# Two more k-tile pairs with seven block products in the down projection, and the first gain moved behind them

## The chip, the cores and the metric

The kernel runs on one core of one Trainium2 chip. The metric is the device time of one execution in microseconds (us); three runs of the kernel before gave 2082.16, 2082.45 and 2082.65 us, median 2082.45. The profile is of a further execution that took 2081.73 us, of which 2079.9 us lie between its first and its last instruction (the span).

## The reference, cut to what matters

One decoder layer on 256 tokens with a model width of 2048: a SwiGLU feed-forward block (FFN), token mixing, and a second FFN. The change is in the FFN, which runs twice with different weights:

```
D_MODEL, SEQ, D_FF = 2048, 256, 5632

def rmsnorm(x, g):
    return x * rsqrt(mean(x * x) + EPS) * g

def swiglu(x, wg, wu, wd):
    return (silu(x @ wg) * (x @ wu)) @ wd      # wd: 5632 x 2048

f = swiglu(rmsnorm(h, pre_g), wg, wu, wd)
h = h + 0.5 * rmsnorm(f, post_g)
```

All is float32. The part `... @ wd` is called the down stage here.

## The kernel before, in words

**Three passes for one product.** Each float32 operand is split in two parts for TensorE, a rounded one (`_hi`) and the rest (`_lo`), and a product takes three matmuls: hi by hi, lo by hi, hi by lo. ScalarE (ACT) makes the rounded part of a weight slab (`hi`, L517: `whi<-raw`), VectorE (DVE) the rest of it (`lo`, L957: `wlo<-raw,whi`), and TensorE (PE) takes both (`slab`, L1544).

**Slabs and the ring.** A weight slab is two k-tiles of 128 rows by 512 columns, 512 KB. `raw`, `whi` and `wlo` have four slots each, so a load may start when `lo` of the slab four back is done, and `hi` of a slab must wait until PE has used the slab four back (`mm_done`).

**The down stage.** The 5632 hidden rows are 44 k-tiles, or 22 k-tile pairs, numbered q. The 2048 output columns are four chunks of 512. The first half of the stage takes chunks 0 and 1 with q from 0 to 21, two slabs for each q; the second half takes chunks 2 and 3. I number the slabs of the stage from 0 in the order of loading, so q = 20 and q = 21 of the first half are slabs 40 to 43, and the second half starts with slab 44.

**Seven products in place of eight.** For one q, two token tiles by two column chunks by two k-tiles are eight block products of three matmuls, 24 in all. For the q in `DOWN_SEVEN` (9, 11, ..., 19) a scheme of the Strassen-Winograd kind does with seven, 21 matmuls. For that it needs sums of the activations (`down_sum`, split in `down_hi` and `down_lo`, made once for each q and used in both halves) and sums of the weights: four additions on DVE (`weight_sums`, L1150 to L1155), the rounded part on ACT (`wsum_hi`, L688) and the rest on DVE (`down_wsum_lo`, L1159). Four of the seven products go to extra banks (M1, M5, M6, M7), and after the last such q `outer_copies` (ACT, L693 and L694), `combine` (DVE, L1165 to L1171) and `combine_last` (DVE, L1177) put them together in `comb`.

**The order in the second half.** `FRONT` lists the q that are taken for both chunks together: 0, then a plain q and a seven in turn, (1, 9), (2, 11), ..., (6, 19), so 13 of them. `REST` holds the other nine. They are taken for chunk 2 and then for chunk 3, one slab each; the last four slabs of chunk 3 are taken by token tile (`last_slabs`).

**The gain.** The two finished chunks 0 and 1 wait in `comb`. `gain` (DVE, L1245) multiplies them by `gpost` into `fout`, and `squares_of` (ACT, L700) squares them in place for the norm. In the kernel before that is done at i = 3 to 6 of `FRONT`. `comb` must be free before `outer_copies(1)` writes it.

**What sets the order.** Each engine has its own instruction list, written out by hand, and works through it in that order. An engine that waits on a semaphore holds back all that stands behind. No scheduler moves anything.

Of the kernel before, what the change touches and what calls it, by code (L numbers as in the profile page):

```python
# [40 lines left out]
SK = 2  # L41
# [45 lines left out]
SEVEN = (1, 3, 5)  # L87
SUMMED = UP_CHUNKS - 1
DOWN_SEVEN = (9, 11, 13, 15, 17, 19)
PLAIN = [q for q in range(DOWN_SLABS) if q not in DOWN_SEVEN]  # L90
FRONT = PLAIN[:1] + [q for two in zip(PLAIN[1:], DOWN_SEVEN) for q in two]
REST = [q for q in PLAIN if q not in FRONT]
HALF_SLABS = 2 * DOWN_SLABS
REST2, REST3 = HALF_SLABS + 2 * len(FRONT), HALF_SLABS + 2 * len(FRONT) + len(REST)
CONVERT = {0: (0,), 1: (1,), 2: (2,), 3: (3, 4), 4: (5,), 5: (6,), 6: (7,), 7: (8,), 8: (9,), 10: (10,)}
SEVENS = len(SEVEN) * SUMMED + 2 * len(DOWN_SEVEN)
ASUMS = len(SEVEN) + len(DOWN_SEVEN)
COMBINES = SUMMED + 2
SCRATCH = 2048
M1, M5, M6, M7 = range(4)  # L100
# [5 lines left out]
def build(nc, x, rel_bias, f1_wg, f1_wu, f1_wd, f1_post, w_in, b_gate, w_o, conv_dw,  # L106
# [6 lines left out]
    with ctx:  # L113
# [389 lines left out]
        def _(act):  # L503
# [100 lines left out]
            def ffn(f):  # L604
# [71 lines left out]

                def quad(half, n, q):

                    if q in DOWN_SEVEN:
                        seven = down_seven(f, half, DOWN_SEVEN.index(q))  # L680
                    hi_at(n)
                    if q in DOWN_SEVEN:
                        act.wait_ge(wsum_ready, 4 * seven + 3)
                    hi_at(n + 1)
                    if q in DOWN_SEVEN:
                        act.wait_ge(wsum_ready, 4 * seven + 4)
                        act.wait_ge(wsum_used, seven)
                        nc.scalar.activation(wsum_hi[:], wsum[:], ACT.Copy).then_inc(wsumhi_ready, 1)  # L688

                def outer_copies(half):  # L690

                    act.wait_ge(wsum_used, down_seven(f, half, len(DOWN_SEVEN)))
# [10 lines left out]
                for q in range(DOWN_SLABS):  # L703
                    for c in CONVERT.get(q, ()):
                        act.wait_ge(hf_ready, UP_CHUNKS * f + c + 1)
                        nc.scalar.activation(h_hi[:, KB * c:KB * c + KB, :], h_f[:, KB * c:KB * c + KB, :],
                                             ACT.Copy).then_inc(hhi_ready, 1)
                    quad(0, 2 * q, q)
                    if q == 1:
                        gate_silu(SUMMED)  # L710
                    if q == 5:
                        hidden_copy(SUMMED, 0)
                    for c in CONVERT.get(q, ()):
                        if 2 * c + 1 in DOWN_SEVEN:
                            i = DOWN_SEVEN.index(2 * c + 1)
                            act.wait_ge(asum_ready, ASUMS * f + len(SEVEN) + i + 1)
                            nc.scalar.activation(down_hi[:, i], down_sum[:, i], ACT.Copy).then_inc(asumhi_ready, 1)
                    if q == DOWN_SEVEN[-1] + 1:
                        outer_copies(0)
                for i, q in enumerate(FRONT):  # L720
                    quad(1, HALF_SLABS + 2 * i, q)
                    if i == 4:
                        squares_of(0, C11)
                    if i == 6:
                        squares_of(1, C12)
                for k in range(len(REST)):
                    hi_at(REST2 + k)
                    if k == 1:
                        outer_copies(1)
                for k in range(len(REST)):  # L730
                    hi_at(REST3 + k)
# [212 lines left out]
        def _(dve):  # L944
# [162 lines left out]
            def ffn(f):  # L1107
# [117 lines left out]
                def hidden_sums_lo(c):  # L1225
# [23 lines left out]

                def quad(half, n, q, between=None):  # L1250

                    if q in DOWN_SEVEN:
                        seven = down_seven(f, half, DOWN_SEVEN.index(q))
# [288 lines left out]
        def _(pe):  # L1542
# [88 lines left out]
            def ffn(f):  # L1631
# [352 lines left out]
```

## Time and profile before

| | us | |
|---|---|---|
| profiled execution | 2081.73 | span 2079.9 |
| PE busy | 2067.6 | 99% of the span, 9322 matmul records |
| PE weight load | 1711.2 | 82%, lies beside the matmuls |
| DVE busy | 1680.6 | 81% |
| ACT busy | 1111.2 | 53% |
| mean granted PE clock | | 0.999 |
| chain that ended last | | PE 95%, of it L1544 (all the products) 93% |

The busy times overlap. The chain is the work that ended last, followed back step by step to what released it. PE takes up almost all of it.

### The profile page before, as it was taken

What the parts mean: (1) busy time and instruction counts of PE and PEld (TensorE: products, weight loads), DVE (VectorE), ACT (ScalarE), POOL (GpSimd) and SP (SyncE); (2) the same over time, 40 slices, a digit from 0 to 9 for tenths busy, and PEclk for the clock granted to TensorE, in tenths of its full rate; (3) what the DMA queues carried; (4) which work ended last, traced back from release to release, by engine and by line L of the source; (5) the groups of instructions that cost most, each with busy time, mean ns of one, the idle gap of its engine ahead of it and who ended that gap; (6) DMA issues with size and microseconds to landing.
All of it is one profiled execution on the core that took longest, in us unless ns stands there. A gap on an engine that the chain in (4) does not pass through costs nothing.

```text
span 2079.9 us, 25938 instructions
## 1 busy us (share of the span) xinstructions
PE 2067.6 (99%) x9322; PEld 1711.2 (82%) x9322; DVE 1680.6 (81%) x2049; ACT 1111.2 (53%) x1252; POOL 27.7 (1%) x54
## 2 busy tenths in 40 slices
PE   9999999999999999999999999999999999999998
PEld 8888888888888788888788888888888888888886
DVE  6889889889887658998687555578898888889885
ACT  6555555556555454444556444465555555565453
POOL 0000000000000000100000000000000000000000
PEclk9999999999999999999999999999999999999999
DMA  8666556666666566776655666556566665656564
GB/s 287 220 200 205 192 191 202 202 201 193 203 195 215 171 185 191 207 202 179 177 175 175 187 191 209 192 174 208 187 202 201 202 202 187 209 190 208 197 202 162
DMA packets 211996, 409.51 MB, mean 197 GB/s; under 512 B 15114, under 2 KB 15378, under 8 KB 211521
## 3 DMA queue, kind: packets, MB, share of 16 engines
q1 hardware_dynamic: 209904, 401.26, 60.4%
q0 software_dynamic: 1856, 7.01, 1.4%
q8 instruction: 56, 0.92, 0.2%
q14 instruction: 36, 0.29, 0.0%
q10 hardware_dynamic: 144, 0.04, 0.0%
HBM read 406.14 MB, written 2.11 MB: 196 GB/s over the span
## 4 chain that ended last, share of the span: by engine, by line
PE 95%; DVE 2%; DMA 1%; issue 1%; ACT 0%; SPq 0%; POOL 0%; DVEq 0%; ACTq 0%; POOLq 0%
PE banks L1544 93%; PE banks L1594 2%; DVE wlo L957 1%; DMA raw<-in_ffn_wu_dram 1%; DVE res L1012 0%; DMA raw<-in_ffn_wg_dram 0%; DVE act_lo L1025 0%; DVE wsum L1150 0%; DVE wsum L1155 0%; ACT act_hi L532 0%; ACT whi L517 0%; DVE nat L1138 0%; POOL stat L430 0%; DVE comb L1169 0%; DVE comb L1165 0%
## 5 line engine op out<-in xcount | busy, mean ns | idle before, releaser
L517 ACT ACTIVATE whi<-raw 128x1024 fp32r<-128x1024 f32 x755 | 779.7, 1053 | 734.6 <-PE banks L1544 372.1
L957 DVE TENSOR_TENSOR wlo<-raw,whi 128x1024 fp32r<-128x1024 f32 x756 | 900.2, 1218 | 258.9 <-ACT whi L517 255.8
L1544 PE MATMUL banks<-whi,act_hi 128*128 128x512 f32 x1688 | 541.7, 395 | 0.8 <-DVE wlo L957 0.7
L1544 PE MATMUL banks<-whi,act_lo 128*128 128x512 f32 x1688 | 532.0, 389 | 0.0
L1544 PE MATMUL banks<-wlo,act_hi 128*128 128x512 f32 x1688 | 522.3, 389 | 0.1
L1544 PEld LDWEIGHTS banks<-whi,act_lo 128*128 128x128 f32 x1688 | 316.9, 188 | 66.8
L1544 PEld LDWEIGHTS banks<-wlo,act_hi 128*128 128x128 f32 x1688 | 316.7, 188 | 66.7 <-DVE wlo L957 1.0
L1544 PEld LDWEIGHTS banks<-whi,act_hi 128*128 128x128 f32 x1688 | 313.6, 188 | 67.2 <-issue 4.7
L1544 PE MATMUL banks<-whi,h_hi 128*128 128x512 f32 x560 | 179.2, 390 | 0.0
L1544 PE MATMUL banks<-whi,h_lo 128*128 128x512 f32 x560 | 179.0, 389 | 0.0
L1544 PE MATMUL banks<-wlo,h_hi 128*128 128x512 f32 x560 | 174.9, 389 | 0.0
L1544 PEld LDWEIGHTS banks<-whi,h_lo 128*128 128x128 f32 x560 | 105.2, 188 | 21.9
L1544 PEld LDWEIGHTS banks<-wlo,h_hi 128*128 128x128 f32 x560 | 105.1, 188 | 21.7
L1544 PEld LDWEIGHTS banks<-whi,h_hi 128*128 128x128 f32 x560 | 105.0, 188 | 21.6
L1159 DVE TENSOR_TENSOR wsum_lo<-wsum,wsum_hi 128x1536 fp32r<-128x1536 f32 x60 | 105.2, 1753 | 0.0
L1316 DVE SCALAR_TENSOR_TENSOR conv_out<-conv_in,dwt,conv_out 128x256 f32<-128x256 f32 x240 | 100.4, 482 | 0.0
L656 ACT ACTIVATE wsum_hi<-wsum 128x1536 fp32r<-128x1536 f32 x60 | 88.4, 1473 | 0.0
L1150 DVE TENSOR_TENSOR wsum<-raw 128x512 f32<-128x512 f32 x84 | 58.0, 690 | 34.3 <-DMA raw<-in_ffn_wu_dram 18.9
L1152 DVE TENSOR_TENSOR wsum<-wsum,raw 128x512 f32<-128x512 f32 x84 | 58.1, 692 | 2.9
L642 ACT ACTIVATE h_f<-banks 128x1024 f32 (+1 forms) x22 | 22.6, 1025 | 67.8 <-PE banks L1594 67.8
L1165 DVE TENSOR_TENSOR comb<-comb,banks 128x512 f32<-128x512 f32 x24 | 16.5, 688 | 52.1 <-ACT comb L666 40.7
L1155 DVE TENSOR_TENSOR wsum<-wsum,raw 128x512 f32<-128x512 f32 x84 | 57.5, 685 | 0.0
(239 smaller groups left out, 2017.7 us busy)
## 6 DMA issues: line engine op xcount, KB each, us to landing
raw<-in_ffn_wg_dram SPq DMA_DIRECT2D x176, 512.0 KB, 3.7
raw<-in_ffn_wu_dram SPq DMA_DIRECT2D x176, 512.0 KB, 4.6
raw<-in_ffn_wd_dram SPq DMA_DIRECT2D x176, 512.0 KB, 4.7
raw<-in_w_in_dram SPq DMA_DIRECT2D x160, 512.0 KB, 3.6
raw<-in_w_out_dram SPq DMA_DIRECT2D x32, 512.0 KB, 3.6
raw<-in_w_pw_dram SPq DMA_DIRECT2D x16, 512.0 KB, 3.7
raw<-in_w_o_dram SPq DMA_DIRECT2D x16, 512.0 KB, 3.7
x_t<-in_x_tiles_dram SPq DMA_DIRECT2D x8, 256.0 KB, 6.7
```

The costliest lines, as they stand in the source:

```text
L517: nc.scalar.activation(whi[:, j % RING, 0:kts * width], raw[:, j % RING, 0:kts * width], ACT.Copy).then_inc(hi_ready, 1)
L642: nc.scalar.activation(h_f[:, bass.ds(KB * c, KB), :], spare_blocks(group), ACT.Copy).then_inc(hf_ready, 1)
L656: nc.scalar.activation(wsum_hi[:], wsum[:], ACT.Copy).then_inc(wsumhi_ready, 1)
L957: nc.vector.tensor_tensor(wlo[:, j % RING, 0:n], raw[:, j % RING, 0:n], whi[:, j % RING, 0:n], ALU.subtract).then_inc(lo_ready, 1)
L1150: nc.vector.tensor_tensor(wsum[:, P_SUM, :], b11, b12, ALU.add).then_inc(wsum_ready, 1)
L1152: nc.vector.tensor_tensor(wsum[:, R_SUM, :], wsum[:, P_SUM, :], b22, ALU.add).then_inc(wsum_ready, 1)
L1155: nc.vector.tensor_tensor(wsum[:, Z_SUM, :], wsum[:, R_SUM, :], b21, ALU.add).then_inc(wsum_ready, 1)
L1159: nc.vector.tensor_tensor(low[:], wsum[:], wsum_hi[:], ALU.subtract).then_inc(wsumlo_ready, 1)
L1165: nc.vector.tensor_tensor(comb[:, C12, :], comb[:, C11, :], banks[:, b + M6, :], ALU.add).then_inc(combined, 1)
L1316: ins = nc.vector.scalar_tensor_tensor(out=dst, in0=src, scalar=dwt[:, c, w:w + 1], in1=dst, op0=ALU.mult, op1=ALU.add)
L1544: return nc.tensor.matmul(o, a, b, **kw)
L1594: ins = nc.tensor.transpose(dst[:, block0 + k, t * P:(t + 1) * P], src[:, t, k * P:(k + 1) * P], ident[:])
```

## The change

For the second half of the columns only, q = 5 and q = 7 are taken with seven products too, after the six that were. Their activation sums get new buffers (`extra_sum`, `extra_hi`, `extra_lo`, and `extra_full` for hi plus lo of the hidden rows) in the memory that `fout` of chunks 0 and 1 uses. They are made during q = 20 and q = 21 of the first half. `FRONT` grows from 13 to 17 (its new end is 10, 5, 12, 7) and `REST` shrinks from nine to five (14, 16, 18, 20, 21). Gain and squares of chunks 0 and 1 move behind the last seven, into `REST`, and `combine` from the second to the fourth slab of `REST`.

```diff
+EXTRA = (5, 7)
+SEVEN_OF = (DOWN_SEVEN, DOWN_SEVEN + EXTRA)
-PLAIN = [q for q in range(DOWN_SLABS) if q not in DOWN_SEVEN]
-FRONT = PLAIN[:1] + [q for two in zip(PLAIN[1:], DOWN_SEVEN) for q in two]
+PLAIN = [q for q in range(DOWN_SLABS) if q not in SEVEN_OF[1]]
+FRONT = PLAIN[:1] + [q for two in zip(PLAIN[1:], SEVEN_OF[1]) for q in two]
...
@@ scalar (ACT), first half, at the end of the loop over q
                     if q == DOWN_SEVEN[-1] + 1:
                         outer_copies(0)
+                    if q >= DOWN_SLABS - len(EXTRA):
+                        i = q - DOWN_SLABS + len(EXTRA)
+                        act.wait_ge(asum_ready, ASUMS * f + len(SEVEN) + len(DOWN_SEVEN) + i + 1)
+                        nc.scalar.activation(extra_hi[:, i], extra_sum[:, i], ACT.Copy).then_inc(asumhi_ready, 1)
                 for i, q in enumerate(FRONT):
                     quad(1, HALF_SLABS + 2 * i, q)
-                    if i == 4:
-                        squares_of(0, C11)
-                    if i == 6:
-                        squares_of(1, C12)
                 for k in range(len(REST)):
                     hi_at(REST2 + k)
-                    if k == 1:
+                    if k == 2:
+                        squares_of(0, C11)
+                        squares_of(1, C12)
+                        act.wait_ge(squared, 2 * TT * BLK * f + 2 * TT)
                         outer_copies(1)
...
@@ vector (DVE)
+                def extra_sums(i):
+                    q = EXTRA[i]
+                    link(nc.vector.tensor_tensor(extra_full[:, i], h_hi[:, SK * q:SK * q + SK, :], h_lo[:, SK * q:SK * q + SK, :],
+                                                 ALU.add))
+                    a11, a12, a21, a22 = (extra_full[:, i, k, t * P:(t + 1) * P] for t in range(TT) for k in range(2))
+                    link(nc.vector.tensor_tensor(extra_sum[:, i, S5, :], a21, a22, ALU.subtract))
+                    nc.vector.tensor_tensor(extra_sum[:, i, S7, :], a11, a21, ALU.subtract)
+                    link(nc.vector.tensor_tensor(extra_sum[:, i, S6, :], extra_sum[:, i, S5, :], a11, ALU.subtract))
+                    nc.vector.tensor_tensor(extra_sum[:, i, S3, :], extra_sum[:, i, S6, :], a12, ALU.add).then_inc(asum_ready, 1)
+
+                def extra_sums_lo(i):
+                    dve.wait_ge(asumhi_ready, ASUMS * f + len(SEVEN) + len(DOWN_SEVEN) + i + 1)
+                    nc.vector.tensor_tensor(extra_lo[:, i], extra_sum[:, i], extra_hi[:, i], ALU.subtract).then_inc(asumlo_ready, 1)
...
                     if q == DOWN_SEVEN[-1] + 1:
                         combine(SUMMED + 1, 1)
+                    if q >= DOWN_SLABS - len(EXTRA):
+                        extra_sums(q - DOWN_SLABS + len(EXTRA))
                 dve.wait_ge(gpost_full, 16 if f == 0 else 48)
                 for i, q in enumerate(FRONT):
                     quad(1, HALF_SLABS + 2 * i, q,
                          (lambda: combine_last(SUMMED + 1, 1, down0 + HALF_SLABS)) if i == 2 else None)
-                    if i == 3:
-                        gain(0, C11)
-                    if i == 5:
-                        gain(1, C12)
+                    if i < len(EXTRA):
+                        extra_sums_lo(i)
                 for k in range(len(REST)):
                     lo_at(REST2 + k)
                     if k == 1:
+                        dve.wait_ge(wsum_used, down_seven(f, 1, len(SEVEN_OF[1])))
+                        gain(0, C11)
+                        gain(1, C12)
+                    if k == 3:
                         combine(SUMMED + 2, 0)
```

The rest of the diff replaces `DOWN_SEVEN` by `SEVEN_OF[half]` where a q is looked up, and gives PE `extra_hi` and `extra_lo` for the two new q.

**ScalarE where the first half ends, before:** L688 is `wsum_hi` of q = 19, L693 and L694 are `outer_copies(0)`, and the eight L517 that follow are `whi` of slabs 42 to 49.

```order
L688 ACTIVATE wsum_hi<-wsum 128x1536
L517 ACTIVATE whi<-raw 128x1024 x2
L693 ACTIVATE comb<-banks 128x512
L694 ACTIVATE comb<-banks 128x512
L517 ACTIVATE whi<-raw 128x1024 x8
L688 ACTIVATE wsum_hi<-wsum 128x1536
```

The same place of the changed kernel, where L524 is `whi`, L695 `wsum_hi`, L700 and L701 the outer copies, and L730 the rounded part of the new sums:

```order
L695 ACTIVATE wsum_hi<-wsum 128x1536
L524 ACTIVATE whi<-raw 128x1024 x2
L700 ACTIVATE comb<-banks 128x512
L701 ACTIVATE comb<-banks 128x512
L730 ACTIVATE extra_hi<-extra_sum 128x512
L524 ACTIVATE whi<-raw 128x1024 x2
L730 ACTIVATE extra_hi<-extra_sum 128x512
L524 ACTIVATE whi<-raw 128x1024 x6
```

An `extra_hi` now stands ahead of `whi` of slab 42, and another ahead of `whi` of slab 44.

**ScalarE around the last seven of the second half, before:** L700 are squares (two for a chunk), L693 and L694 `outer_copies(1)`, and the eleven L517 `whi` of `REST` from its third slab on.

```order
L688 ACTIVATE wsum_hi<-wsum 128x1536
L517 ACTIVATE whi<-raw 128x1024 x2
L693 ACTIVATE comb<-banks 128x512
L694 ACTIVATE comb<-banks 128x512
L517 ACTIVATE whi<-raw 128x1024 x11
L700 ACTIVATE comb,fsq<-comb 128x512 x2
L517 ACTIVATE whi<-raw 128x1024 x5
```

The same place of the changed kernel, where L707 are the squares:

```order
L695 ACTIVATE wsum_hi<-wsum 128x1536
L524 ACTIVATE whi<-raw 128x1024 x3
L707 ACTIVATE comb,fsq<-comb 128x512 x4
L700 ACTIVATE comb<-banks 128x512
L701 ACTIVATE comb<-banks 128x512
L524 ACTIVATE whi<-raw 128x1024 x6
L707 ACTIVATE comb,fsq<-comb 128x512 x2
L524 ACTIVATE whi<-raw 128x1024
```

Four squares now stand between the third `whi` of `REST` and the outer copies, and six slabs instead of eleven lie between the outer copies and the squares of chunk 2.

## Rows read from the trace of the kernel before

**Rows 1.** The page, part 1: busy us, share of the span, instructions.
```profile
PE 2067.6 (99%) x9322; PEld 1711.2 (82%) x9322; DVE 1680.6 (81%) x2049; ACT 1111.2 (53%) x1252; POOL 27.7 (1%) x54
```
**Rows 2.** Waits of PE: us in total, times, longest us.
```profile
PE banks L1594 <- DVE res L1012: 1.8, 2, 1.6
...
PE banks L1544 <- DVE wlo L957: 0.7, 2, 0.4
```
**Rows 3.** Timeline of PE: start, duration, engine, line; slabs 40, 42, 48 and 52.
```profile
580.73 0.62 PE L1544 MATMUL banks<-whi,h_hi 128*128 128x512 f32 x2
...
586.17 0.62 PE L1544 MATMUL banks<-whi,h_hi 128*128 128x512 f32 x2
...
602.49 0.39 PE L1544 MATMUL banks<-whi,h_hi 128*128 128x512 f32 x1
...
612.69 0.39 PE L1544 MATMUL banks<-whi,h_hi 128*128 128x512 f32 x1
```
**Rows 4.** Timeline of ACT, first FFN: first outer copy, then `whi` of slabs 42 to 44.
```profile
580.93 0.60 ACT L693 ACTIVATE comb<-banks 128x512 f32<-128x512 f32 x1 [3.64 <-PE banks L1544]
...
581.90 2.95 ACT L517 ACTIVATE whi<-raw 128x1024 fp32r<-128x1024 f32 x3
```
**Rows 5.** Timeline of DVE, first FFN: combine's first, `wlo` 42 to 45, weight sums 48, `combine_last`.
```profile
582.05 0.69 DVE L1165 TENSOR_TENSOR comb<-comb,banks 128x512 f32<-128x512 f32 x1 [2.59 <-ACT comb L694]
...
584.84 4.62 DVE L957 TENSOR_TENSOR wlo<-raw,whi 128x1024 fp32r<-128x1024 f32 x4
...
595.71 0.69 DVE L1150 TENSOR_TENSOR wsum<-raw 128x512 f32<-128x512 f32 x1 [0.64 <-DMA raw<-in_ffn_wd_dram]
...
598.25 2.28 DVE L1177 TENSOR_TENSOR comb<-comb,banks 128x2048 f32<-128x2048 f32 x1
600.45 2.35 DVE L957 TENSOR_TENSOR wlo<-raw,whi 128x1024 fp32r<-128x1024 f32 x2
```
**Rows 6.** Timeline of PE, second FFN: slab 40.
```profile
1945.40 0.62 PE L1544 MATMUL banks<-whi,h_hi 128*128 128x512 f32 x2
```
**Rows 7.** Timeline of ACT, second FFN: `whi` of slabs 42 to 44.
```profile
1946.57 2.96 ACT L517 ACTIVATE whi<-raw 128x1024 fp32r<-128x1024 f32 x3
```
**Rows 8.** Timeline of DVE: sums like the new ones, in the up stage, and what follows.
```profile
30.08 0.69 DVE L1113 TENSOR_TENSOR afull<-act_hi,act_lo 128x512 f32<-128x512 f32 x1
...
31.65 0.29 DVE L1118 TENSOR_TENSOR asum<-asum,afull 128x128 f32<-128x128 f32 x1
31.86 1.22 DVE L957 TENSOR_TENSOR wlo<-raw,whi 128x1024 fp32r<-128x1024 f32 x1
```
**Rows 9.** Timeline of ACT: rounded part of the sums of q = 9.
```profile
490.37 0.63 ACT L717 ACTIVATE down_hi<-down_sum 128x512 fp32r<-128x512 f32 x1 [1.38 <-DVE down_sum L1223]
490.91 1.04 ACT L706 ACTIVATE h_hi<-h_f 128x1024 fp32r<-128x1024 f32 x1
```
**Rows 10.** Timeline of DVE: a `wlo` that PE waits for.
```profile
708.40 1.22 DVE L957 TENSOR_TENSOR wlo<-raw,whi 128x1024 fp32r<-128x1024 f32 x1 [0.34 <-ACT whi L517]
```
**Rows 11.** Timeline of PE: the matmul that waited for it.
```profile
709.77 0.47 PE L1544 MATMUL banks<-whi,act_hi 128*128 128x512 f32 x1 [0.33 <-DVE wlo L957]
```
**Rows 12.** Timeline of DVE, both FFNs: `wlo` of a seven, next weight sums.
```profile
641.34 2.35 DVE L957 TENSOR_TENSOR wlo<-raw,whi 128x1024 fp32r<-128x1024 f32 x2
...
648.93 0.69 DVE L1150 TENSOR_TENSOR wsum<-raw 128x512 f32<-128x512 f32 x1 [1.30 <-DMA raw<-in_ffn_wd_dram]
...
1994.49 2.35 DVE L957 TENSOR_TENSOR wlo<-raw,whi 128x1024 fp32r<-128x1024 f32 x2
...
2001.35 0.69 DVE L1150 TENSOR_TENSOR wsum<-raw 128x512 f32<-128x512 f32 x1 [0.57 <-DMA raw<-in_ffn_wd_dram]
```
**Rows 13.** Instructions on `comb`: count, ns min/median/max.
```profile
L700 ACT ACTIVATE comb<-comb x12: 610/617/634, 612.5 to 2051.8; 128x512 f32<-128x512 f32 x12
...
L1245 DVE TENSOR_TENSOR fout<-comb,gpost x6: 1217/1218/1221, 606.7 to 2049.9; 128x1024 f32<-128x1024 f32 x6
```
**Rows 14.** Timeline of PE: the kernel's first matmuls.
```profile
1.54 5.57 PE L1544 MATMUL banks<-ident 128*128 128x128 f32 x26 [1.54 <-POOL ident L421]
```

More of the change, by code:

```diff
@@ L95 @@
 CONVERT = {0: (0,), 1: (1,), 2: (2,), 3: (3, 4), 4: (5,), 5: (6,), 6: (7,), 7: (8,), 8: (9,), 10: (10,)}
-SEVENS = len(SEVEN) * SUMMED + 2 * len(DOWN_SEVEN)
-ASUMS = len(SEVEN) + len(DOWN_SEVEN)
+SEVENS = len(SEVEN) * SUMMED + len(SEVEN_OF[0]) + len(SEVEN_OF[1])
+ASUMS = len(SEVEN) + len(SEVEN_OF[1])
 COMBINES = SUMMED + 2
@@ L156, in build @@
         o_dsum = o_act + 4 * TT * 2 * CW
+        extra_hi, o_ehi = sb("extra_hi", [P, len(EXTRA), 4, P], f32r, over=o_act)
+        extra_lo, o_elo = sb("extra_lo", [P, len(EXTRA), 4, P], f32r, over=o_act + 16 * P * len(EXTRA))
+        extra_full, _ = sb("extra_full", [P, len(EXTRA), SK, SEQ], over=o_ehi)
+        extra_sum, _ = sb("extra_sum", [P, len(EXTRA), 4, P], over=o_elo)
+        assert o_elo + 16 * P * len(EXTRA) <= o_dsum
         down_hi, _ = sb("down_hi", [P, len(DOWN_SEVEN), 4, P], f32r, over=o_dsum)
@@ L677, in quad @@
                 def quad(half, n, q):
-                    if q in DOWN_SEVEN:
-                        seven = down_seven(f, half, DOWN_SEVEN.index(q))
+                    if q in SEVEN_OF[half]:
+                        seven = down_seven(f, half, SEVEN_OF[half].index(q))
                     hi_at(n)
-                    if q in DOWN_SEVEN:
+                    if q in SEVEN_OF[half]:
                         act.wait_ge(wsum_ready, 4 * seven + 3)
                     hi_at(n + 1)
-                    if q in DOWN_SEVEN:
+                    if q in SEVEN_OF[half]:
                         act.wait_ge(wsum_ready, 4 * seven + 4)
@@ L690, in outer_copies @@
                 def outer_copies(half):
-                    act.wait_ge(wsum_used, down_seven(f, half, len(DOWN_SEVEN)))
+                    act.wait_ge(wsum_used, down_seven(f, half, len(SEVEN_OF[half])))
                     nc.scalar.activation(comb[:, C11, :], banks[:, 4 * half + M1, :], ACT.Copy)
@@ L1250, in quad @@
                 def quad(half, n, q, between=None):
-                    if q in DOWN_SEVEN:
-                        seven = down_seven(f, half, DOWN_SEVEN.index(q))
+                    if q in SEVEN_OF[half]:
+                        seven = down_seven(f, half, SEVEN_OF[half].index(q))
                         weight_sums(seven, (down0 + n) // RING + 1, n % RING, False)
@@ L1258, in quad @@
                     lo_at(n + 1)
-                    if q in DOWN_SEVEN:
+                    if q in SEVEN_OF[half]:
                         weight_sums_lo(seven, down_wsum_lo)
@@ L1726, in quad @@
                 def quad(half, n, q):
-                    if q in DOWN_SEVEN:
-                        i = DOWN_SEVEN.index(q)
+                    if q in SEVEN_OF[half]:
+                        i = SEVEN_OF[half].index(q)
                         acts = [[k_tile(t, 2 * q + k, m) for t in (h_hi, h_lo)] for m, k in ((0, 0), (0, 1), (1, 1))]
+                        if q in EXTRA:
+                            sums = [t[:, EXTRA.index(q)] for t in (extra_hi, extra_lo)]
+                        else:
+                            sums = [t[:, i] for t in (down_hi, down_lo)]
                         pe.wait_ge(asumlo_ready, ASUMS * f + len(SEVEN) + i + 1)
                         seven_products(down_seven(f, half, i), down0 + n + 1, n % RING, 1 - half, i == 0,
-                                       i == len(DOWN_SEVEN) - 1, acts, [down_hi[:, i], down_lo[:, i]], down_wsum_lo)
+                                       i == len(SEVEN_OF[half]) - 1, acts, sums, down_wsum_lo)
                     else:
```

## Prediction

> **What bounds the kernel now.** I read the busy times first. PE has 2067.6 of 2079.9 us [rows 1]. The list of waits of PE then tells how little it waits for others: 0.7 us for `wlo`, 1.8 us for `res`, the longest 1.6 us [rows 2]. So the kernel is bound by the number of matmuls, and two questions decide: how many go, and whether PE, which now hardly waits, begins to.
>
> The rate of PE comes from its timeline. Slab 48 starts at 602.49, slab 52 at 612.69 [rows 3]. Between them lie 21 matmuls of a seven and 24 of a plain q: 10.20 / 45 = 0.2267 us each. A slab of 12 takes 2.72 us. Slab 40 starts at 580.73 and slab 42 at 586.17, 5.44 us for two slabs, the same rate [rows 3].
>
> **What goes.** Two q in each FFN, three matmuls in each: 2 x 2 x 3 = 12 matmuls, 12 x 0.2267 = 2.72 us. PE never waits in this stretch, so all of it would be gained if it still doesn't.
>
> **What is added in the middle of the stage, step by step (first FFN).** Before the change ACT makes the outer copies from 580.93 to 581.90 and goes straight on to `whi` of slabs 42, 43 and 44: three in 2.95 us, so 1.05 for one and 0.95 from start to start [rows 4]. PE needs the first at 586.17, over 3 us later: this is its cover. Now the rounded part `extra_hi` stands ahead of that `whi`, and waits for sums that DVE makes only after `combine`.
>
> 1. `combine` begins at 582.05 and frees DVE at 584.84 [rows 5]. It can't be earlier, as it needs the outer copies, and these need the end of PE's last seven at 580.73.
> 2. The new sums have the shape of the sums in the up stage: from 30.08 to 31.65 + 0.29 they take 1.86 us, and the next instruction starts after 1.78 [rows 8]. They end at 584.84 + 1.86 = 586.70.
> 3. `extra_hi` starts some 0.05 later and occupies ACT for 490.91 - 490.37 = 0.54 us [rows 9]. So ACT starts `whi` 42 at 587.29 and ends it at 588.35.
> 4. A matmul that waited for DVE started 709.77 - (708.40 + 1.22) = 0.15 us after its releaser's end [rows 10, 11]. PE starts slab 42 at 588.50, not 586.17: a wait of 2.33 us.
> 5. `wlo` 42 can't start before 588.4. It ends at 589.61 and reaches PE at 589.76, which is through its first four matmuls at 588.50 + 0.91 = 589.41: 0.35 us more. Sum 2.68.
> 6. The second set goes the same way, but PE now comes later too. DVE does `wlo` 43, then the sums until about 592.55; `extra_hi` and `whi` 44 end at 594.2, when PE, 2.68 late, is at slab 44 (586.17 + 5.44 + 2.68 = 594.29). Nearly no wait for `whi`, 0.36 for `wlo` 44 as in step 5. Sum 3.07 with 0.03 for `whi`.
>
> All these steps hang on the end of PE's last seven, and the second FFN has the same distances: PE starts slab 40 at 1945.40, ACT `whi` 42 at 1946.57 [rows 6, 7], 1.17 after it in both. So they count twice: 2 x 3.07 = 6.1 us. The new `extra_lo` (two of the shape of `down_lo`, under a `wlo` of 1.22 us) stand where DVE waits for loads anyway; I give them nothing, and 0.7 us each if that cover is gone.
>
> **What is late next: the load for the first seven of the second half.** The `raw` of slab 49 is asked for when `wlo` 45 is done. Before, that was at 584.84 + 4.62 = 589.46, and the weight sums of 48/49 started at 595.71, released by the DMA, 6.25 us later [rows 5]. Now `wlo` 45 ends at about 596.6. How long the load takes then isn't shown; the bounds are 6.25 us for four loads asked for in a burst, and 4.51 (2001.35 - 1996.84, second FFN) and 5.24 (648.93 - 643.69, first FFN) for the usual pair [rows 12]. Here only two are asked for close together, so I take the pair's value of each FFN. The weight sums and `combine_last` take 600.45 - 595.71 = 4.74 us from start to next [rows 5] (4.82 to the end), and PE waits for `combine_last` before slab 48. First FFN: 596.6 + 5.24 + 4.82 + 0.15 = 606.8, PE is there at 602.49 + 3.07 = 605.56: wait 1.2. Second FFN: 0.5. With 6.25 it would be 2.2 in either, below 4.0 nothing. Then `wlo` 48 comes 0.23 late behind `combine_last`. Sum of this step: 1.2 + 0.5 + 2 x 0.23 = 2.2 us, bounds 0.5 and 4.9.
>
> In the pairs that follow, DVE and the loads need 4.89 us (4.74 less 2.20 for `combine_last` up to the next start, plus 2.35 for two `wlo`, rows 5) and then 4.51 to 5.24, so 9.4 to 10.1 us, against 10.20 for PE. No further growth; but in a pair where the load takes over 5.3 us PE would wait, as it has no spare time left. I add 0.2 for the first FFN.
>
> **What is moved to the end of the stage.** Gains, squares and outer copies now stand in one chain behind PE's last seven, whose end I call T: gain 1.22 and a second beside the first squares, then four squares of some 0.6 us [rows 13], outer copies 0.97 (580.93 to 581.90, rows 4), `whi` and `wlo` of the fourth slab of `REST`, `combine` 2.79 [rows 5] and `wlo` of the fifth, which reaches PE at about T + 11.4. PE needs it at T + 4 x 2.72 + 0.91 = T + 11.8: covered by 0.4 us. Before, nothing but `combine` stood there. Next, chunk 2 ends at T + 13.6: addition 1.2, `wlo`, gain 1.2, squares 1.2, `whi` 1.05, `wlo` 1.22 for the last slab; with the starts before the ends this gives T + 21.0, while PE, after five slabs of chunk 2, one of chunk 3 and three tiles of six matmuls (1.36 us each), is there at T + 20.4. Before, `REST` was four slabs longer and all this lay under it. I put 0.6 us in each FFN, 1.2 in sum; bounds 0 and 2.6 (1.3 each, if DVE also comes to the end of the pairs without its lead). That `FRONT` no longer holds two gains on DVE and four squares on ACT gains nothing while PE isn't waiting for them.
>
> **The sum.** -2.7 + 6.1 + 2.2 + 0.2 + 1.2 = +7.0 us. Against the profiled execution: 2081.73 + 7.0 = 2088.7 us. The median of the three runs, 2082.45, is 0.7 above that execution, which gives 2089.4. I write 2089.0. About 0.2%, 4.2 us, is what a measurement of this kernel can tell from no change.
>
> **Rivals.**
>
> *A, the forecast* (ACT held by the wait for the sums): own range 2086.8 to 2091.5, chance 0.60.
>
> *B, the loads don't recover* (chance 0.12). PE comes out of the middle of the stage with no lead, and each of the seven remaining pairs of the second half costs 0.2 to 0.4 us, if the loads take 5.5 us or more. For it: they took over 5.2 us in the first FFN. Against it: 4.5 in the second [rows 12], and DVE has lost the gains. Price: the middle load at its upper bound, +2.7, and 14 x 0.2 = 2.8: 2091.5 to 2094.5.
>
> *C, the waits are covered* (chance 0.05 for this, 0.17 for the part below). PE has work ahead of it, and all additions disappear: 2082.45 - 2.7 = 2079.7, not slower than before. The place is slab 42. It decides by whether ACT starts its `whi` by 586.17 - 0.15 - 1.05 = 584.97. For it speaks that ACT is busy only 53% [rows 1]. Against it: DVE is in `combine` until 584.84 [rows 5] and the sums take 1.86, so ACT is free 2.3 us too late. *C2*: only steps 4 and 5 hold, and loads and tail are covered: 2 x 2.7 - 2.7 = +2.7, 2085.1, no measurable change; chance 0.17.
>
> *D, the clock falls* (chance 0.06). PE has not stood still for more than 1.6 us after the start [rows 2], with a mean granted clock of 0.999; now it stands for 2.3 and again soon. If it fell to the lower of its two levels (1.2 in place of 2.4 GHz) for a stretch like that at the start, where 26 short matmuls took 5.57 us [rows 14], each FFN would lose half of such a stretch, 2.8 us: 2089 + 5.6 = 2094.6. The Trainium skill speaks for this one: "TensorE: Matmul & The Clock Gate", section "What's actually happening", says that "the default state is throttled, and activity releases the throttle". The trace of before has no wait long enough to test it; by that rule the sum would be D's, by the waits that the rows do show, without a drop, it stays at A's.
>
> **How the numbers follow.** Slower by over 0.2% are A, B and D: 0.78. Within 0.2% is C2: 0.17. Faster is C: 0.05. The range reaches from C2's value to the middle of B and the edge of D: 2084.8 to 2093.8; outside lie C and the most of D, some of B.
>
> **What would show it.** In the timeline of the changed kernel, `extra_hi` of q = 5 should begin 6.0 us after PE's slab 40 with ACT idle until then, released by DVE's sums, and PE should show a wait of 2.3 us for `whi` before slab 42, in both FFNs. PE should wait for `combine_last` before slab 48, more in the first FFN. The list of waits of PE should grow from some 4 us to about 13. The matmul records should be 12 fewer than 9322. If PE shows no wait at slab 42, the forecast is wrong at its main step; if the granted clock falls below 0.99, D is at work.

## The result, and the profile after

| | before | changed |
|---|---|---|
| median, us | 2082.42 (2081.70 to 2082.65, 6 runs) | 2090.72 (2089.54 to 2091.59, 6 runs) |
| ratio, 95% interval | | 1.004 (1.0029 to 1.0052) |
| profiled execution, us | 2081.73, span 2079.9 | 2090.99, span 2089.1 |

The change costs 8.3 us; 7.0 were forecast. 2090.72 is 1.7 us above the 2089.0 written down and inside the stated range, outside the 0.2% that can't be told from no change, and on the side that was given 0.78.

The page shows the 12 matmuls gone, and DVE with 25 us more to do:

```profile
PE 2070.5 (99%) x9310; PEld 1708.3 (82%) x9310; DVE 1705.4 (82%) x2093; ACT 1118.4 (54%) x1260; POOL 27.7 (1%) x54
```

PE's busy time has not fallen with the number of matmuls [rows 1]. The record of a matmul is 0.39 us long where the next one starts after 0.2267 us, so a wait of up to 0.16 us doesn't show as idle time. And matmuls that run slower, as some do below, fill more time. So a share of 99% says nothing here. The list of waits does (us in total, times, longest us), which answers to [rows 2]:

```profile
PE banks L1574 <- ACT whi L524: 4.0, 2, 2.0
PE banks L1624 <- DVE res L1022: 1.9, 2, 1.6
PE banks L1574 <- POOL ident L428: 1.5, 1, 1.5
PE banks L1574 <- DVE wlo L967: 1.5, 4, 0.4
PE banks L1574 <- DVE comb L1187: 0.8, 2, 0.5
PE banks L1574 <- DVE act_lo L1035: 0.6, 1, 0.6
```

The first line is new: two waits of 2.0 us for `whi`. So is the one for L1187, `combine_last`. The list has grown from 4.0 to 10.3 us, not to the 13 that were forecast. It leaves out the first 0.16 us of each wait, and all the small ones. Starts of matmuls leave out nothing, so the shares below are taken from them. The timeline of ACT shows why (start, duration, engine, line; first FFN, as [rows 4]):

```profile
581.42 0.60 ACT L700 ACTIVATE comb<-banks 128x512 f32<-128x512 f32 x1 [3.64 <-PE banks L1574]
581.91 0.59 ACT L701 ACTIVATE comb<-banks 128x512 f32<-128x512 f32 x1
587.22 0.63 ACT L730 ACTIVATE extra_hi<-extra_sum 128x512 fp32r<-128x512 f32 x1 [4.71 <-DVE extra_sum L1250]
587.75 1.99 ACT L524 ACTIVATE whi<-raw 128x1024 fp32r<-128x1024 f32 x2
593.00 0.63 ACT L730 ACTIVATE extra_hi<-extra_sum 128x512 fp32r<-128x512 f32 x1 [3.26 <-DVE extra_sum L1250]
```

ACT stands idle for 4.71 us between the outer copies and `extra_hi`, with `whi` of slab 42 behind it. The timeline of DVE at the same place, as [rows 5], has the sums behind `combine`, then `wlo` 42 waiting for `whi`, later `wlo` 44, the weight sums of slab 48 and `combine_last`:

```profile
585.32 0.69 DVE L1244 TENSOR_TENSOR extra_full<-h_hi,h_lo 128x512 f32<-128x512 f32 x1
...
586.89 0.29 DVE L1250 TENSOR_TENSOR extra_sum<-extra_sum,extra_full 128x128 f32<-128x128 f32 x1
588.83 2.36 DVE L967 TENSOR_TENSOR wlo<-raw,whi 128x1024 fp32r<-128x1024 f32 x2 [1.64 <-ACT whi L524]
...
594.69 2.36 DVE L967 TENSOR_TENSOR wlo<-raw,whi 128x1024 fp32r<-128x1024 f32 x2 [1.72 <-ACT whi L524]
...
602.89 0.69 DVE L1160 TENSOR_TENSOR wsum<-raw 128x512 f32<-128x512 f32 x1 [2.36 <-DMA raw<-in_ffn_wd_dram]
...
605.43 2.28 DVE L1187 TENSOR_TENSOR comb<-comb,banks 128x2048 f32<-128x2048 f32 x1
```

The timeline of PE, as [rows 3] (slab 40, slab 42 up to its neighbour, slab 48), shows both waits and something between them:

```profile
581.22 0.62 PE L1574 MATMUL banks<-whi,h_hi 128*128 128x512 f32 x2
...
588.85 0.73 PE L1574 MATMUL banks<-whi,h_hi 128*128 128x512 f32 x2 [2.03 <-ACT whi L524]
589.42 0.78 PE L1574 MATMUL banks<-whi,h_lo 128*128 128x512 f32 x2
590.11 1.22 PE L1574 MATMUL banks<-wlo,h_hi 128*128 128x512 f32 x2
591.12 1.05 PE L1574 MATMUL banks<-whi,h_hi 128*128 128x512 f32 x2
591.98 1.05 PE L1574 MATMUL banks<-whi,h_lo 128*128 128x512 f32 x2
592.83 0.77 PE L1574 MATMUL banks<-wlo,h_hi 128*128 128x512 f32 x2
593.44 0.63 PE L1574 MATMUL banks<-whi,h_hi 128*128 128x512 f32 x2
...
607.76 0.50 PE L1574 MATMUL banks<-whi,h_hi 128*128 128x512 f32 x1 [0.52 <-DVE comb L1187]
```

From slab 40 to slab 42 it takes 588.85 - 581.22 = 7.63 us instead of 5.44: 2.19 us late. Then two matmuls take 0.86 us (591.12 to 591.98) in place of 0.45. The busy times by stretch have the granted clock in the column behind POOL; the first three stretches are of the first FFN, the last two of the second:

```profile
585.00:590.00 5.00, 2.97 (x13) 1.84 (x11) 3.26 (x8) 2.53 (x3) 0.00 (x0) 0.97 0.00 0
590.00:595.00 5.00, 5.00 (x16) 3.96 (x16) 3.18 (x8) 2.00 (x3) 0.00 (x0) 0.69 0.58 178
595.00:600.00 5.00, 5.00 (x23) 4.13 (x23) 5.00 (x6) 2.54 (x3) 0.00 (x0) 1.00 0.58 176
...
1955.00:1960.00 5.00, 2.98 (x13) 1.95 (x11) 3.26 (x7) 2.52 (x3) 0.00 (x0) 1.00 0.00 0
1960.00:1965.00 5.00, 4.93 (x22) 3.87 (x22) 3.18 (x8) 1.89 (x3) 0.00 (x0) 1.00 0.63 205
```

In the first FFN 16 matmuls fit where otherwise 23 do, at a mean clock of 0.69. It fell to the lower of its two levels (1.2 GHz) for some 3 us. The mean of 0.97 up to 590.00 puts the fall at about 589.7, so PE, which had stood for 2.2 us, was at work again since 588.85. In the second FFN the same stand of PE was followed by no fall. PE there, slabs 42 and 48, and the weight sums of 48:

```profile
1958.96 0.73 PE L1574 MATMUL banks<-whi,h_hi 128*128 128x512 f32 x2 [2.02 <-ACT whi L524]
...
1976.66 0.50 PE L1574 MATMUL banks<-whi,h_hi 128*128 128x512 f32 x1 [0.31 <-DVE comb L1187]
```
```profile
1964.80 2.36 DVE L967 TENSOR_TENSOR wlo<-raw,whi 128x1024 fp32r<-128x1024 f32 x2 [1.72 <-ACT whi L524]
...
1971.79 0.69 DVE L1160 TENSOR_TENSOR wsum<-raw 128x512 f32<-128x512 f32 x1 [1.15 <-DMA raw<-in_ffn_wd_dram]
```

PE's starts at the same slabs in both traces give where the 9.2 us between the two spans arise. Slab 40 of the second FFN starts at 1951.34 in the changed kernel.

| stretch | us later, first FFN | second FFN |
|---|---|---|
| slab 40 to 42 | 2.19 | 2.18 |
| slab 42 to 48 | 2.59 | 1.38 |
| slab 48 to the stage's end | 0.34 | -0.30 |

That is 8.4 us. The last row holds the gain of 1.36 us from the six matmuls, so 1.70 and 1.06 us of waits are in it: 0.6 in each FFN where PE first needs the last slab of chunk 3, the rest nearly all `wlo` in the sevens. The other 0.8 us lie outside the changed code: 0.49 before the first slab 40, where this execution's PE waited 0.6 us for `act_lo` at its start, and 0.33 between the FFNs.

### The profile page after: what moved, and what is told of

The parts are those of the page before. It is cut to its first block, busy times and chain, and to the rows that moved or that the text cites. A ratio compares the mean times of both kernels' runs of the same rounds, so it can differ in the third digit from the quotient of the medians.

```text
span 2089.1 us, 25982 instructions
## 1 busy us (share of the span) xinstructions
PE 2070.5 (99%) x9310; PEld 1708.3 (82%) x9310; DVE 1705.4 (82%) x2093; ACT 1118.4 (54%) x1260; POOL 27.7 (1%) x54
## 4 chain that ended last, share of the span: by engine, by line
PE 90%; DVE 5%; DMA 3%; ACT 1%; issue 1%; POOL 0%; SPq 0%; DVEq 0%; ACTq 0%; POOLq 0%
PE banks L1574 88%; DMA raw<-in_ffn_wd_dram 2%; DVE wlo L967 2%; PE banks L1624 2%; ACT whi L524 0%; DVE res L1022 0%; DMA raw<-in_ffn_wg_dram 0%; DVE wsum L1160 0%; DVE wsum L1162 0%; DVE wsum L1165 0%; DVE comb L1187 0%; DVE raw L1163 0%; ACT comb L707 0%; DVE act_lo L1035 0%; DVE fout L1271 0%
## 5 line engine op out<-in xcount | busy, mean ns | idle before, releaser
L524 ACT ACTIVATE whi<-raw 128x1024 fp32r<-128x1024 f32 x755 | 779.4, 1053 | 726.5 <-PE banks L1574 347.3
L1574 PE MATMUL banks<-whi,h_hi 128*128 128x512 f32 x536 | 173.7, 392 | 5.6 <-ACT whi L524 4.0
L1574 PE MATMUL banks<-whi,h_lo 128*128 128x512 f32 x536 | 172.9, 390 | 0.0
L1574 PE MATMUL banks<-wlo,h_hi 128*128 128x512 f32 x536 | 169.2, 392 | 0.1
L1574 PEld LDWEIGHTS banks<-whi,h_hi 128*128 128x128 f32 x536 | 100.5, 188 | 28.8 <-ACT whi L524 4.9
L1574 PEld LDWEIGHTS banks<-wlo,h_hi 128*128 128x128 f32 x536 | 100.5, 189 | 23.6 <-DVE wlo L967 3.3
L1574 PEld LDWEIGHTS banks<-whi,h_lo 128*128 128x128 f32 x536 | 100.9, 188 | 21.1
L1162 DVE TENSOR_TENSOR wsum<-wsum,raw 128x512 f32<-128x512 f32 x88 | 60.9, 692 | 3.0
L1163 DVE TENSOR_TENSOR raw<-raw 128x512 f32<-128x512 f32 x88 | 60.2, 684 | 0.0
L1165 DVE TENSOR_TENSOR wsum<-wsum,raw 128x512 f32<-128x512 f32 x88 | 60.2, 684 | 0.0
```

What stands on the lines that cost most here:

```text
L524: nc.scalar.activation(whi[:, j % RING, 0:kts * width], raw[:, j % RING, 0:kts * width], ACT.Copy).then_inc(hi_ready, 1)
L1162: nc.vector.tensor_tensor(wsum[:, R_SUM, :], wsum[:, P_SUM, :], b22, ALU.add).then_inc(wsum_ready, 1)
L1163: nc.vector.tensor_tensor(b12, b12, b22, ALU.add).then_inc(wsum_ready, 1)
L1165: nc.vector.tensor_tensor(wsum[:, Z_SUM, :], wsum[:, R_SUM, :], b21, ALU.add).then_inc(wsum_ready, 1)
L1574: return nc.tensor.matmul(o, a, b, **kw)
```

## The experiments

The theory: ScalarE is held in front of slab 42 by a semaphore, the wait reaches PE, and all that follows (late loads, a tail with no cover, perhaps the clock) comes on top. The rivals: the new work on DVE itself, the two new sevens, the move of the gain. Each kernel is the changed one with the edit shown. Where a share of PE's delay is given, it is the time between the starts of matmuls beyond 0.2267 us each.

**ScalarE's part alone moved (e1_act_late).**

```diff
@@ scalar, end of the first half, then the second
-                    if q >= DOWN_SLABS - len(EXTRA):
-                        i = q - DOWN_SLABS + len(EXTRA)
-                        act.wait_ge(asum_ready, ASUMS * f + len(SEVEN) + len(DOWN_SEVEN) + i + 1)
-                        nc.scalar.activation(extra_hi[:, i], extra_sum[:, i], ACT.Copy).then_inc(asumhi_ready, 1)
                 for i, q in enumerate(FRONT):
                     quad(1, HALF_SLABS + 2 * i, q)
+                    if 0 <= i - 0 < len(EXTRA):
+                        e = i - 0
+                        act.wait_ge(asum_ready, ASUMS * f + len(SEVEN) + len(DOWN_SEVEN) + e + 1)
+                        nc.scalar.activation(extra_hi[:, e], extra_sum[:, e], ACT.Copy).then_inc(asumhi_ready, 1)
```

> The changed kernel with one edit: ScalarE makes the rounded part of each new sum (extra_hi) after its slabs 44/45 and 46/47, not before slabs 42 and 44. VectorE still makes the sums where the change put them. Theory (ScalarE held in front of the weight slabs is the main cost): PE's 2.2 us wait for whi before slab 42 goes in both FFNs, and with it any fall of the clock; left are about 1.0 us per FFN for wlo of slab 42, behind the sums on VectorE, and the tail of 0.6 us. Time 2082.4 - 2.7 + 2.0 + 1.2 = 2082.9 us, 2082.2 to 2084.2. Rival (VectorE's sums and the late loads behind them are the cost, ScalarE only waits along): the waits at slabs 42 and 48 stay and the time is over 2088.

Measured: 2083.99 us (2083.39 to 2084.42, 11 runs), 6.7 us less than the changed kernel; ratio to before 1.0007 (0.9998 to 1.0016). PE's waits:

```profile
PE banks L1574 <- DVE wlo L967: 2.8, 6, 0.7
...
PE banks L1574 <- DVE comb L1187: 0.5, 1, 0.5
```

The wait for `whi` is gone. What is left at slab 42 is 0.81 us for `wlo`, in each FFN. It now starts at 586.83, behind the sums:

```profile
585.05 0.68 DVE L1244 TENSOR_TENSOR extra_full<-h_hi,h_lo 128x512 f32<-128x512 f32 x1
...
586.83 2.35 DVE L967 TENSOR_TENSOR wlo<-raw,whi 128x1024 fp32r<-128x1024 f32 x2
```

The changed kernel loses 11.0 us in waits and slow matmuls, its 8.3 and the 2.7 that the sevens should give. The place of the two `extra_hi` in ScalarE's list accounts for 6.7 of them. The rest is the sums' place on VectorE (slabs 42 to 48) and the tail. The time is 1.1 us above the point expected and in the stated range; the wait of 0.5 for `combine_last` wasn't in it.

**Sums, rounding and rests in the second half (e2_sums_late).**

```diff
@@ vector
-                    if q >= DOWN_SLABS - len(EXTRA):
-                        extra_sums(q - DOWN_SLABS + len(EXTRA))
@@ vector, second half
                     if i < len(EXTRA):
-                        extra_sums_lo(i)
+                        extra_sums(i)
+                    if 0 <= i - 3 < len(EXTRA):
+                        extra_sums_lo(i - 3)
```

ScalarE's part is that of e1, one place later (i = 1 and 2).

> Sums, rounded parts and rests all moved into the second half: VectorE makes the sums after slabs 44/45 and 46/47, where it waited for loads before, ScalarE rounds them after slabs 46/47 and 48/49, the rests come after slabs 50/51 and 52/53. Theory: no wait of PE at slabs 42 to 48, the 12 matmuls are gained, the tail of 0.6 us per FFN stays: 2082.4 - 2.7 + 1.2 = 2080.9 us, 2080.2 to 2081.8. Rival (the additional VectorE work does not fit anywhere before the first seven of the half, since weight sums and combine_last come late behind it): PE waits for combine_last before slab 48 by 0.5 to 1.5 us per FFN, 2082 to 2084 us.

Measured: 2082.06 us (2080.64 to 2083.39, 11 runs), ratio 0.9998 (0.9989 to 1.0007). The median is 1.2 us above the point and outside the theory's range; as a time it lies where the rival had it, 2082 to 2084. The profile doesn't show the rival's wait: PE waits neither at slab 42 nor for `combine_last` before slab 48. It has the tail waits as expected (0.6 in each FFN) and small waits of 0.1 each for `wlo` in the first two sevens of the first FFN's second half. The profiled execution took 2081.18 us, so what the slower ones had on top is not shown.

**The tail alone (e3_tail).**

```diff
@@ scalar
                     hi_at(REST2 + k)
-                    if k == 2:
+                    if k == 3:
                         squares_of(0, C11)
...
                     hi_at(REST3 + k)
-                    if k == 3:
+                    if k == 4:
                         squares_of(2, C11)
```

> The changed kernel with only the end of the down stage altered: ScalarE makes whi of the fourth slab of REST before the squares, and whi of the last slab of chunk 3 before the squares of chunk 2. Theory (a tail wait of 0.5 us per FFN at the last slab, because its whi stands behind squares that wait for the gain): the wait of PE for wlo before its last tile of six goes, 2090.7 - 1.2 = 2089.5 us, and the waits at slabs 42 and 48 stay. Rival (the tail wait is due to the shorter REST, whatever ScalarE's order): no change, 2090.7.

Measured: 2089.01 us (2088.55 to 2090.26, 6 runs), 1.7 less than the changed kernel, 1.2 expected. The two sets of runs overlap, so the place of the wait is the better witness. In the changed kernel ACT did the last `whi` of the stage behind the squares:

```profile
702.28 0.63 ACT L707 ACTIVATE comb<-comb 128x512 f32<-128x512 f32 x1 [0.58 <-DVE fout L1271]
...
703.53 1.04 ACT L524 ACTIVATE whi<-raw 128x1024 fp32r<-128x1024 f32 x1
```

With the edit it is ahead of them, as soon as PE frees the slot, and PE's wait there is gone in both FFNs:

```profile
699.96 1.06 ACT L524 ACTIVATE whi<-raw 128x1024 fp32r<-128x1024 f32 x1 [1.66 <-PE banks L1574]
700.93 0.61 ACT L707 ACTIVATE comb<-comb 128x512 f32<-128x512 f32 x1
```

The rival, that the shorter `REST` is to blame whatever the order, is out. The edit moves the squares at two places; which of them counts was not tried apart.

**Both (e4_both).** The edits of e2 and e3 together.

> The sums of e2 and the tail of e3 together. Theory: all added waits are gone and only the 12 matmuls' gain is left: 2082.4 - 2.7 = 2079.7 us, 2079.3 to 2080.4, so the seven products are worth 2.7 us when nothing waits. Rival (a matmul less is not a time less, since the loads or VectorE bound the pairs of the second half): 2081.5 or more, with PE waiting for wlo in the pairs.

Measured: 2080.61 us (2079.43 to 2081.08, 11 runs), ratio 0.999 (0.9981 to 0.9999). It is faster than before by 1.8 us; 2.7 were expected, and the time lies 0.2 above the stated range. Its profile still has about 0.9 us of small waits for `wlo` in the first FFN, 0.1 to 0.15 each, in three of the sevens: with the sums among them, DVE has less lead there. In this the rival has its share, a small one. e8 below, with the sums elsewhere, has none of these waits.

**The move alone (e5_moved_only).** No new sevens and no sums; gain, squares and `combine` stay where the change put them.

```diff
-SEVEN_OF = (DOWN_SEVEN, DOWN_SEVEN + EXTRA)
+SEVEN_OF = (DOWN_SEVEN, DOWN_SEVEN)
```

The instructions of `extra_hi`, `extra_sums` and `extra_sums_lo` are taken out of ScalarE's and VectorE's lists.

> Only the move: gain and squares of chunks 0 and 1 and combine stand behind the sevens as in the changed kernel, but no new sevens and no new sums (FRONT 13, REST nine slabs as before). Theory (the move alone is covered by a REST of nine slabs): 2082.4 us, within 0.5. Rival (gain, squares and outer copies in one chain hold back PE whatever the length of REST): a wait of PE for wlo of 0.5 us or more per FFN, 2083.4 or more.

Measured: 2082.03 us (2081.60 to 2082.74, 11 runs), ratio 0.9998 (0.9989 to 1.0007). PE has no wait in the second half of the down stage that the kernel before didn't have. The move costs nothing while `REST` is nine slabs long.

**The sums made, not used (e6_unused).** As e5, but the sums, their rounded parts and rests are made where the change put them; all q of the second half but the six old ones take eight products.

```diff
-SEVEN_OF = (DOWN_SEVEN, DOWN_SEVEN + EXTRA)
+SEVEN_OF = (DOWN_SEVEN, DOWN_SEVEN)
-ASUMS = len(SEVEN) + len(SEVEN_OF[1])
+ASUMS = len(SEVEN) + len(DOWN_SEVEN) + len(EXTRA)
```

> The changed kernel with the new sums made and split as in it, but not used: q = 5 and q = 7 are taken with eight products, so 12 matmuls more than the changed kernel and 9322 in all. Theory (the waits at slabs 42 to 48 come from the sums' place in the lists and stay; the seven products' gain of 2.7 us is missing, the tail wait of 1.0 us too, since REST is nine slabs long): 2090.7 + 2.7 - 1.0 = 2092.4 us, 2091.5 to 2093.5. Rival (part of the loss comes from the two new sevens, whose weight sums load VectorE and the loads in the pairs): less than 2091.

Measured: 2091.65 us (2090.68 to 2091.95, 5 runs), ratio 1.0043 (1.0029 to 1.0057). That is 9.2 us over before, without a single new seven, and at the lower end of the stated range. Of the changed kernel's 11.0 us only 1.8 are missing. The tail makes 1.2 of them, so 0.6 or so are left for the rival, the new sevens themselves. PE's waits, and the clock in both FFNs:

```profile
PE banks L1574 <- ACT whi L524: 4.0, 2, 2.0
...
PE banks L1574 <- DVE comb L1187: 1.1, 1, 1.1
```
```profile
590.00:595.00 5.00, 4.95 (x22) 3.74 (x21) 3.18 (x8) 1.75 (x3) 0.00 (x0) 1.00 0.58 171
...
1960.00:1965.00 5.00, 5.00 (x15) 4.03 (x16) 3.18 (x7) 2.11 (x3) 0.00 (x0) 0.67 0.66 209
```

Here the clock fell in the second FFN and not in the first. In the first, without the fall, PE waits 1.31 us before slab 48, against 1.2 in the forecast. From slab 42 at 589.09 to slab 48 at 607.67 it loses 18.58 - 16.32 = 2.26 us (six slabs take 16.32).

The traces of three kernels have the same work up to slab 48, so they can be compared there. The load is the time from the end of `wlo` 45 to the weight sums of 48:

| kernel, FFN | fall of the clock | load, us | lost from slab 42 to 48, us |
|---|---|---|---|
| changed, first | yes | 5.84 | 2.59 |
| changed, second | no | 4.63 | 1.38 |
| e3, first | yes | 4.62 | 2.09 |
| e3, second | no | 4.95 | 1.71 |
| e6, first | no | 5.50 | 2.26 |
| e6, second | yes | 4.30 | 2.06 |

In the three rows without a fall the loss is the load less 3.24 or 3.25 us, whatever the FFN. With a fall it is 2.1 us or that same difference, whichever is more.

**The sums made twice (e7_doubled).**

```diff
                 def extra_sums(i):
...
                     link(nc.vector.tensor_tensor(extra_full[:, i], h_hi[:, SK * q:SK * q + SK, :], h_lo[:, SK * q:SK * q + SK, :],
                                                  ALU.add))
+                    link(nc.vector.tensor_tensor(extra_full[:, i], h_hi[:, SK * q:SK * q + SK, :], h_lo[:, SK * q:SK * q + SK, :],
+                                                 ALU.add))
                     a11, a12, a21, a22 = (extra_full[:, i, k, t * P:(t + 1) * P] for t in range(TT) for k in range(2))
+                    link(nc.vector.tensor_tensor(extra_sum[:, i, S5, :], a21, a22, ALU.subtract))
+                    nc.vector.tensor_tensor(extra_sum[:, i, S7, :], a11, a21, ALU.subtract)
+                    link(nc.vector.tensor_tensor(extra_sum[:, i, S6, :], extra_sum[:, i, S5, :], a11, ALU.subtract))
+                    link(nc.vector.tensor_tensor(extra_sum[:, i, S3, :], extra_sum[:, i, S6, :], a12, ALU.add))
...
```

> The changed kernel with each set of new sums on VectorE made twice, 1.8 us more in front of each extra_hi. Theory for the hold: PE's wait for whi before slab 42 grows from 2.2 to 4.0 us in both FFNs and one of about 1.8 us appears before slab 44; without any further loss of clock the time is 2090.7 + 4 x 1.8 = 2097.9 us less up to 1.0 for what the waits at slab 48 took. Theory for the clock (a longer stand of PE brings the lower clock in both FFNs, not only in the first): matmuls of 0.43 us start to start after slab 42 in both FFNs, and 1.7 us or more on top, 2099 to 2103. Rival (the lower clock in the first FFN had nothing to do with the wait): granted clock 1.00 in the second FFN, 2096.9 to 2097.9.

Measured: 2096.46 us (2096.26 to 2099.37, 4 runs), ratio 1.0071 (1.0056 to 1.0087). PE's waits and the clock:

```profile
PE banks L1580 <- ACT whi L524: 8.9, 4, 3.9
```
```profile
590.00:595.00 5.00, 4.23 (x12) 3.38 (x13) 4.15 (x6) 1.67 (x2) 0.00 (x0) 0.66 0.33 87
...
1960.00:1965.00 5.00, 2.64 (x7) 2.06 (x8) 3.33 (x6) 2.52 (x3) 0.00 (x0) 0.77 0.04 10
```

At slab 42 PE is 4.09 us late in both FFNs, as expected (2.19 + 1.8 = 4.0), and the clock falls in both. But the median missed all expectations and lies below each of them: PE waits only 0.75 and 0.60 us at slab 44, not 1.8. A slower PE comes later to the next slab, and the wait there shrinks. The two losses don't add.

**The same work in idle time (e8_idle_place).** The tail of e3, and the sums before `combine` instead of behind it.

```diff
@@ vector, first half
                     if q == DOWN_SEVEN[-1] + 1:
+                        for i in range(len(EXTRA)):
+                            extra_sums(i)
                         combine(SUMMED + 1, 1)
-                    if q >= DOWN_SLABS - len(EXTRA):
-                        extra_sums(q - DOWN_SLABS + len(EXTRA))
```

On ScalarE the first `extra_hi` stands ahead of `outer_copies(0)`, not behind it; the second stays behind `whi` of slab 43.

> The tail of e3, and the new sums at another place of the first half: VectorE makes both before combine, while it waits for PE's last seven, and ScalarE rounds the first before the outer copies and the second after slab 43's whi. The same work, still ahead of slabs 42 and 44. Theory (what counts is that the sums hang on combine, which hangs on PE's last seven; in the idle time before it they cost nothing): waits of 0 to 0.3 us at slab 42, 2080.6 us, 2079.8 to 2081.4. Rival (any extra work in front of slab 42 makes PE wait, as ScalarE and VectorE have no spare time there): 2083 or more.

Measured: 2079.89 us (2079.52 to 2080.84, 11 runs), ratio 0.9989 (0.998 to 0.9998). It is faster than before by 2.5 us, near the lower end of the stated range, and the best of all. Its DVE, then its ACT:

```profile
578.64 0.68 DVE L1244 TENSOR_TENSOR extra_full<-h_hi,h_lo 128x512 f32<-128x512 f32 x1
...
582.22 0.69 DVE L1175 TENSOR_TENSOR comb<-comb,banks 128x512 f32<-128x512 f32 x1
...
585.00 4.62 DVE L967 TENSOR_TENSOR wlo<-raw,whi 128x1024 fp32r<-128x1024 f32 x4
```
```profile
580.53 0.63 ACT L728 ACTIVATE extra_hi<-extra_sum 128x512 fp32r<-128x512 f32 x1 [3.07 <-DVE extra_sum L1250]
581.10 0.60 ACT L700 ACTIVATE comb<-banks 128x512 f32<-128x512 f32 x1
...
582.07 2.01 ACT L524 ACTIVATE whi<-raw 128x1024 fp32r<-128x1024 f32 x2
```

Both sets are done when `combine` may start, and `whi` 42 follows the outer copies at once. PE shows no wait in the whole down stage of either FFN. Nothing was made cheaper: the same sums lie in time in which DVE waited for PE anyway. Against e4 only the place of the sums, their rounded parts and rests is changed. That is worth 0.7 us in the medians, with overlapping runs, and all the small waits for `wlo` in the profile.

## Why the prediction was right

**Slabs 40 to 42, the main step: right.** Forecast 2.33 us for the wait and from ACT's idle time; measured 2.19 in both FFNs, with `extra_hi` 6.0 us after slab 40, as forecast. e1 takes ScalarE's hold away and 6.7 us with it. e6 has the hold without the new sevens and keeps 9.2 us of loss, and e5 shows that the move, which e6 has too, costs nothing.

**Slabs 42 to 48: right in kind, a little low.** Forecast, without `wlo` 48, were 1.94 us in the first FFN and 1.24 in the second, 3.2 in sum; measured 3.97. The term for the load took the usual pair's 5.24 and 4.51 us from the end of `wlo` 45 to the weight sums; it was 602.89 - 597.05 = 5.84 and 1971.79 - 1967.16 = 4.63. That the first FFN has the slower load is not a rule: in e3 it was 4.62 in the first and 4.95 in the second. In e3 the wait before slab 48 is missing in the first FFN. So the step was right, but it was in part luck that the first FFN came out the longer one.

**The clock, rival D: it came, in a smaller size.** It had 0.06 and a price of 5.6 us, as a case of its own. It fell in one FFN of two, and its slow matmuls cost about 1.5 us by themselves, but they lie over waits that PE would have had anyway. By the table under e6 the first FFN would have lost 5.84 - 3.25 = 2.59 us without a fall, and lost 2.59. So in the changed kernel's trace the fall cost nothing net. Where the load was quicker it did cost: an estimate by the same difference is 2.09 - 1.37 = 0.7 us in e3, and 2.06 - 1.05 = 1.0 in e6. The price of 2.8 us for each FFN was too high for two reasons. The slow stretch was some 3 us and not 5.57, and its whole loss was added, although waits lay over it. The step that failed is the sentence that the waits would bring either A or D: both held at once. And the sign for D, a mean clock below 0.99, could not have shown it: the mean was 0.998 with the fall.

**Slab 48 to the end: low by 0.9.** Forecast 0.46 for `wlo` 48, 0.2 for the pairs, 1.2 for the tail, 1.9 in sum; measured 1.70 + 1.06 = 2.8. The tail was right in place and size (0.6 in each FFN; e3 shows it). Mis-sized was `wlo` in the sevens: 0.3 us in the seven of slab 48 of each FFN, where 0.23 were forecast, and 0.2 in each of two later pairs of the first FFN, where 0.2 stood for all. The statement that PE has no lead left there was right.

**Rivals B and C2: neither held.** B had each of seven pairs wait 0.2 to 0.4 us in both FFNs. Two pairs did, in the first FFN alone. C2 had loads and tail covered; PE waited 0.68 and 0.47 us before slab 48, and 0.6 at the tail in each FFN.

**The gain: right.** 2.72 us were taken for the 12 matmuls. e8, where nothing waits, gets 2.5, and its span is 2.3 shorter than before.

**The move: right.** Nothing by itself (e5), only with the shorter `REST` (e3).

**Rival C was wrong** as forecast: ACT's 53% busy share did not help. It was idle for 4.71 us in front of the work that PE needed.

Together the forecast +7.0 stands against +8.3 in the medians, and 8.4 of 9.2 in the changed code by the profiles. The main step was 0.3 us too high and two later ones 0.8 and 0.9 too low, so the errors cancelled little.

## What to carry to other kernels

Before an instruction that waits is put into an engine's list, look at what stands behind it and how long its consumer can do without: here 0.5 us of work on an engine half idle cost 2.2 us, since it waited for a chain that begins when PE ends a step. Look for the idle time ahead of such a chain: the same sums, put before `combine` and not after it, together with the tail's edit (worth 1.2 to 1.7 us by itself), turned +8.3 us into -2.5. And when a loop is shortened, count again what its length used to hide.

## What the runs showed of the hardware

After PE stood for 2.2 us, the granted clock fell to its lower level for about 3 us in one FFN of two: the first one in the changed kernel and in e3, the second one in e6. The two stretches of e3:

```profile
590.00:595.00 5.00, 4.93 (x16) 3.89 (x16) 3.18 (x8) 2.03 (x3) 0.00 (x0) 0.66 0.66 210
...
1960.00:1965.00 5.00, 4.93 (x22) 3.65 (x21) 3.21 (x6) 3.95 (x5) 0.00 (x0) 1.00 0.53 183
```

After 4.1 us it fell in both (e7). After at most 1.8 us, at the start of the stage behind the first FFN, it fell in no trace, nor after the 0.8 us of e1. Which of two equal stands brings it down is not the same in all traces, and what decides that is left open. It may change with each execution of one kernel: the profiled executions have a mean clock of 0.999 without a fall, 0.998 with one and 0.997 with two (e7), and the six of the changed kernel range from 0.997 to 0.999. The one at 0.999 took 2091.36 us and the two at 0.997 took 2089.82 and 2090.45, so fewer falls did not go with a shorter time.

The slow matmuls started 0.43 us apart (591.12 to 591.98 for two) against 0.2267. The Trainium skill ("TensorE: Matmul & The Clock Gate", "What's actually happening") has activity release a throttle that is the default; the fall behind a stand of PE agrees with that. That statement doesn't tell which of two equal stands brings a fall.
